# Bias strips interleaved by four heads, a compressed bias read from them, and a new order of loads and splits in front

## What is computed

```
shift, scale, gate = split(c @ mod_w[0, 0] + mod_b[0, 0])
h    = rms_norm(x, norm_w[0, 0, 0]) * (1 + scale) + shift
proj = h @ w_in_ab          # q, k, v of three branches, gates, q, k, v of the sliding window
# heads a: compressed keys (15), selected blocks, window; summed by gates
s    = q . kc * scale + rel_tab[rel_bucket(t - cmp_end)]    # compressed
s    = q . k  * scale + rel_tab[rel_bucket(t - pos)]        # selected, window
# heads b: sliding window of 128 with a sink logit, same bias, other heads of the table
o    = concat(o_a, o_b) @ w_out_ab
```

## Time and profile before

| | |
|---|---|
| median of the runs | 1017.39 us |
| profiled execution | 1018.37 us, its span 1016.6 us |
| mean granted TensorE clock | 0.986 |
| TensorE busy | 967.5 us (95%) |
| VectorE busy | 799.1 us (79%) |
| ScalarE busy | 557.8 us (55%) |
| DMA | 228.11 MB, mean 224 GB/s |

### The profile page before, as it was taken

How to read it: one execution, slowest core, us unless ns; L and a number is a source line. 1 busy time by engine, 2 the same in 40 slices (tenths; PEclk the granted TensorE clock), 3 DMA queues, 4 the chain that set the end, 5 groups by cost and what they waited for, 6 DMA issues and landing times. The chain is left out here.

```text
span 1016.6 us, 19939 instructions
## 1 busy us (share of the span) xinstructions
PE 967.5 (95%) x7814; PEld 925.4 (91%) x7814; DVE 799.1 (79%) x1436; ACT 557.8 (55%) x1130; POOL 4.8 (0%) x15
## 2 busy tenths in 40 slices
PE   8968989999999999998999999999989899999996
PEld 6757869999999989988999999999888899999995
DVE  4738997798888777888789888877877757877775
ACT  3515874554444465574545444446567457776663
POOL 0100000000000000000000000000000000000000
PEclk9979999999999999999999999999999999999999
DMA  9995776498988756822479888874722436665531
GB/s 345 358 276 178 252 254 249 176 344 321 336 294 295 260 187 219 304 80 99 172 261 330 303 306 302 288 240 183 244 80 73 166 108 185 197 193 186 181 111 42
DMA packets 63004, 228.11 MB, mean 224 GB/s; under 512 B 7091, under 2 KB 7475, under 8 KB 62806
## 3 DMA queue, kind: packets, MB, share of 16 engines
q1 hardware_dynamic: 62150, 224.55, 64.3%
q0 software_dynamic: 640, 2.10, 0.8%
q10 hardware_dynamic: 144, 0.52, 0.1%
HBM read 225.57 MB, written 1.57 MB: 223 GB/s over the span
## 5 line engine op out<-in xcount | busy, mean ns | idle before, releaser
L1935 PE MATMUL bank<-hH,wH 128*128 128x258 f32 (+1 forms) x1520 | 438.0, 288 | 6.7 <-DVE hL L1313 2.6
L1936 PE MATMUL bank<-hL,wH 128*128 128x258 f32 (+1 forms) x1520 | 431.9, 284 | 0.0
L1937 PE MATMUL bank<-hH,wL 128*128 128x258 f32 (+1 forms) x1520 | 430.3, 283 | 0.0
L1266 DVE TENSOR_TENSOR wL<-raw,wH 128x1024 fp32r<-128x1024 f32 x264 | 320.9, 1220 | 43.6 <-ACT wH L780 42.1
L1935 PEld LDWEIGHTS bank<-hH,wH 128*128 128x128 f32 x1520 | 288.8, 190 | 13.0 <-issue 6.2
L780 ACT ACTIVATE wH<-raw 128x1024 fp32r<-128x1024 f32 x264 | 270.2, 1047 | 43.8 <-DMA raw<-in_weights 22.6
L1937 PEld LDWEIGHTS bank<-hH,wL 128*128 128x128 f32 x1520 | 289.9, 191 | 0.0
L1936 PEld LDWEIGHTS bank<-hL,wH 128*128 128x128 f32 x1520 | 289.5, 190 | 0.4
L1935 PE MATMUL bank<-aH,wH 128*128 128x256 f32 x592 | 168.1, 284 | 1.3 <-DVE aL L1499 1.3
L1937 PE MATMUL bank<-aH,wL 128*128 128x256 f32 x592 | 167.6, 283 | 0.0
L1936 PE MATMUL bank<-aL,wH 128*128 128x256 f32 x592 | 167.6, 283 | 0.0
(11 more groups left out here) (335 smaller groups left out, 1038.2 us busy)
## 6 DMA issues: line engine op xcount, KB each, us to landing
raw<-in_weights SPq DMA_DIRECT2D x264, 512.0 KB, 4.6
modbuf<-in_mods SPq DMA_DIRECT2D x129, 512.0 KB, 6.4
raw<-in_mods SPq DMA_DIRECT2D x10, 512.0 KB, 11.8
strips<-bias_table POOLq DMA_DIRECT2D x8, 256.0 KB, 13.5
strips<-in_mods SPq DMA_DIRECT2D x3, 512.0 KB, 15.5
modbuf<-in_weights SPq DMA_DIRECT2D x3, 512.0 KB, 14.0
x<-in_xT SPq DMA_DIRECT2D x2, 512.0 KB, 6.7
proj<-in_mods SPq DMA_DIRECT2D x2, 512.0 KB, 15.0
```

Of the source, the lines that this page charges most:

```text
L1266: V.tensor_tensor(wL[:, slot, :], raw[:, slot, :], wH[:, slot, :].bitcast(F32), ALU.subtract).then_inc(lo_ready[c], 1)
L1935: mm(out, lhs_h, rhs_h, start=start, stop=False, skip_group_check=True)
L1936: mm(out, lhs_h, rhs_l, start=False, stop=False, skip_group_check=True)
L1937: return mm(out, lhs_l, rhs_h, start=False, stop=stop, skip_group_check=True)
```

## The change

1. `strips` goes from 8 x (256 x 2) to 4 x (256 x 4): four heads interleaved, columns of one head 16 bytes apart. The product for the table (68 rows of operand for 34, eight matmuls of 128 columns for four of 256) and POOL's eight DMAs follow (4 runs of 4 KB a partition for 8 of 2 KB).
2. The compressed bias is read from the strips, every 16th column. `hot_cmp`, `relblock`, `cmpmask`, `bc`, their loads, TensorE's 8 products and VectorE's two instructions go. POOL fills `cs` with a large value, where step 3 adds only the valid 7 and 15 columns.
3. SP: `c` and `x` first, then parameters and `rel`; the start's jobs and units in another order; the first part of the constants (with the identity) behind unit 6; `cw_values` no longer wait for the one-hot product and have a semaphore of their own. `warm` (ones) replaces the loaded ones in the first products.
4. ScalarE: the two `crow` copies go to VectorE; the table leaves behind row 4 instead of row 6; POOL's strips wait for job 11, not 15; `split_upto` stands at 8, then 9, for 7, 10, 11 and 12, and `ab_split(s)` is at most 10 + 2s.
5. VectorE: `compressed_input(1, 1)` goes into step 0; units 9 to 11 are split in the steps.
6. TensorE: other numbers and places of clock-keeping matmuls; unit 2's first columns behind those of units 0 and 1.

```diff
-        strips = sb("strips", [P, 8, S, 2])
-        bc = sb("bc", [P, QT, 16, H])
+        strips = sb("strips", [P, 4, S, 4])
...
-            return strips[:, n // 2, cols, n % 2]
+            return strips[:, n // 4, cols, n % 4]
...
-            return min(29, max(e for fill in AB_FILL[:s + 1] for e in fill) + 5)
+            return min(29, 10 + 2 * s, max(e for fill in AB_FILL[:s + 1] for e in fill) + 5)
...
-            sp.dma_start(par[:, 0:PARAM_FIRST], A["params"][:, 0:PARAM_FIRST]).then_inc(par_landed, 16)
             sp.dma_start(crow[0:1, 1, :], A["c"][0:1, :]).then_inc(c_landed, 16)
-            sp.dma_start(con[:, 0:CONST_START], A["consts"][:, 0:CONST_START]).then_inc(con_landed, 16)
-            sp.dma_start(rel, A["rel"]).then_inc(rel_landed, 16)
             for half in range(2):
...
+            sp.dma_start(par[:, 0:PARAM_FIRST], A["params"][:, 0:PARAM_FIRST]).then_inc(par_landed, 16)
+            sp.dma_start(rel, A["rel"]).then_inc(rel_landed, 16)
             load_start_job(0)
+            load_start_job(1)
             load_start_unit(0)
-            load_start_job(1)
             load_start_unit(1)
+            load_start_job(2)
+            load_start_job(3)
             load_start_job(15)
...
             load_unit(6)
-            sp.dma_start(hot_cmp, A["hot_cmp"]).then_inc(hot_landed, 16)
             sp.dma_start(par[:, PARAM_FIRST:], A["params"][:, PARAM_FIRST:]).then_inc(par_landed, 16)
-            sp.dma_start(con[:, CONST_START:CONST_FIRST], A["consts"][:, CONST_START:CONST_FIRST]).then_inc(con_landed, 16)
+            sp.dma_start(con[:, 0:CONST_FIRST], A["consts"][:, 0:CONST_FIRST]).then_inc(con_landed, 16)
...
             jobs_upto(JOBS_END["start"] + 2)
-            sp.wait_ge(misc_psum, misc["bc"] + 1)
...
+            pool.wait_ge(rstd_ready, 1)
+            nc.gpsimd.memset(cs, BIG).then_inc(cs_ready, 1)
+
             pool.wait_ge(table_out, 16)
-            pool.wait_ge(mod_used, JOBS_END["start"])
+            pool.wait_ge(mod_used, 11)
...
-                diag = bass.AP(A["table"].tensor, 2 * (P - 1 - a),
-                               [[8 * 1024 - 2 * 8, COPIES], [1024, 8], [1, 2 * S]])
+                diag = bass.AP(A["table"].tensor, 4 * (P - 1 - a),
+                               [[8 * 1024 - 4 * 8, COPIES], [2048, 4], [1, 4 * S]])
...
+                if k == 4:
+                    act.wait_ge(table_half, 1)
+                    act.wait_ge(misc_taken, misc["table"] + 1)
+                    act.dma_start(A["table"], pt[:, :, :].rearrange("p a b -> p (a b)")).then_inc(table_out, 16)
...
-            split_upto(7)
+            split_upto(8)
             for e in range(2):
                 ab_take(e)
...
-            split_upto(10)
             ab_take(6)
-            split_upto(11)
+            split_upto(9)
             act.wait_ge(misc_psum, misc["gatesT"] + 1)
             nc.scalar.activation(small[:, 0:48], bank[7][:, 0:48], ACT.Exp, scale=-1.0).then_inc(misc_taken, 1)
-            split_upto(12)
             ab_take(7)
...
+            for half in range(2):
+                dve.wait_ge(crow_psum, half + 1)
+                V.tensor_copy(crow[:, 0, half * 512:(half + 1) * 512], bank[(3, 5)[half]][:, :]).then_inc(crow_ready, 1)
+                add_pair(0, half)
...
-            take("bc")
-            dve.wait_ge(con_landed, 32)
-            link(V.tensor_scalar(bc[:, :, :, :].rearrange("p q n h -> p (q n h)"), bank[2][:, 0:S], -1.0, None,
-                                 ALU.mult))
...
-            compressed_input(1, 1)
-            split_upto(11)
             dve.wait_ge(misc_taken, misc["gatesT"] + 1)
...
-            split_upto(12)
+            dve.wait_ge(con_landed, 16)
             dve.wait_ge(strips_landed, 16 * (P // COPIES))
...
+                if s == 0:
+                    compressed_input(1, 1)
...
-                        bias = bc[:, q].rearrange("p n (g t) -> p g t n", g=G)
+                        n = (7, NCMP)[q]
...
+                        at = (1 - q) * P + CLEN - 1
+                        bias = strips[:, 0:G, at:S:CSTR, :].rearrange("p g n t -> p g t n")
                         ins = V.tensor_tensor(dst, src, bias, ALU.add)
...
-            misc_free("bc")
-            keep_clock(bank[2], 6)
+            misc_free("gates")
+            keep_warm(bank[2], 3)
...
-            pe.wait_ge(hot_landed, 16)
-            pe.wait_ge(par_landed, 32)
-            hot = hot_cmp.rearrange("p (g q) -> p g q", g=4)
-            for q in range(QT):
-                for g in range(4):
-                    last = mm(bank[2][:, q * P + g * 32:q * P + (g + 1) * 32], hot[:, g, q * P:(q + 1) * P],
-                              param("relblock"), start=True, stop=True, skip_group_check=True)
-            last.then_inc(misc_psum, 1)
             ab_project(6)
+            misc_free("gates")
```

More of the change, by code:

```diff
@@ L62 @@
 _c = 0
-for _name, _n in (("ident", P), ("ones", P), ("cmpmask", QT * 16), ("rowvalid", QT), ("select", P), ("headmask", H),
+for _name, _n in (("ident", P), ("ones", P), ("rowvalid", QT), ("select", P), ("headmask", H),
                   ("blockones", P), ("rot", P), ("tri", P), ("neg1", P), ("cos", S), ("sin", S),
@@ L150, in shape_constants @@
     put("headmask", (i[:, None] // 16 == np.arange(H)[None]).astype(np.float32))
[L151 to L154, removed]
     far = 255 - np.arange(512)
-    rel = np.zeros((REL + 2, 768), np.float32)
+    rel = np.zeros((REL + 2, 512), np.float32)
     rel[rel_bucket(far), np.arange(512)] = -1.0
-    rel[REL, 0:512] = far < 0
-    rel[REL + 1, 0:512] = far >= 128
-    return c, hot_cmp, rel
+    rel[REL] = far < 0
+    rel[REL + 1] = far >= 128
+    return c, rel
 class Count:
@@ L266, in build_program @@
         ttf = tt.rearrange("p k s -> p (k s)")
[L267 to L268 removed]
+        rel = strips[0:2 * (REL + 2), 0, :, :].rearrange("p s j -> p (s j)")[:, 0:S + 4 * P]
         par_landed = sem("par_landed")
@@ L390, in build_program @@
         NORMS = ["A0", "B0", "A1", "B1", "A2", "B2", "A3", "B3", "A4", "A5", "A6"]
-        MISC = ["table", "bc", "gates", "gatesT", "cmpk", "cmpv", "vrep", "cscore"]
+        MISC = ["table", "gates", "gatesT", "cmpk", "cmpv", "vrep", "cscore"]
         misc = {name: i for i, name in enumerate(MISC)}
@@ L1534, in first_low @@
                                 ALU.subtract).then_inc(h_ready, 1)
-            for b in range(4):
-                add_pair(0, b)
+            add_pair(0, 2)
+            add_pair(0, 3)
             jobs_upto(1)
@@ L1949, in sum_square @@
                     pe.wait_ge(pair_ready, 4 * PAIRED.index(n) + b + 1)
-                    mm(bank[6][:, 0:S], ones, buf[:, 0:S], start=(b == 0), stop=(b == 3),
+                    mm(bank[6][:, 0:S], warm if n == 0 else ones, buf[:, 0:S], start=(b == 0), stop=(b == 3),
                        skip_group_check=True).then_inc(sq_used, 1)
@@ L2183, in _, with keep_warm @@
             pe.wait_ge(warm_ready, 1)
-            for _ in range(5):
-                mm(bank[0][:, 384:512], warm, warm, start=True, stop=True, skip_group_check=True)
-            pe.wait_ge(con_landed, 16)
+            def keep_warm(bk, n):
+                for _ in range(n):
+                    mm(bk[:, 384:512], warm, warm, start=True, stop=True, skip_group_check=True)
+            keep_warm(bank[0], 5)
             pe.wait_ge(c_landed, 16)
             for half in range(2):
-                mm(bank[(3, 5)[half]][:, :], const("ones", 1), crow[0:1, 1, half * 512:(half + 1) * 512], start=True, stop=True,
+                mm(bank[(3, 5)[half]][:, :], warm[0:1, :], crow[0:1, 1, half * 512:(half + 1) * 512], start=True, stop=True,
                    skip_group_check=True).then_inc(crow_psum, 1)
@@ L2193, in _ @@
             for half in range(2):
-                out = bank[(2, 7)[half]][:, :].rearrange("p (n j) -> p n j", j=2)
-                for j in range(2):
-                    last = mm(out[:, :, j], rel[:, 512 + j * P:512 + (j + 1) * P], rel[:, half * S:(half + 1) * S], start=True, stop=True,
+                out = bank[(2, 7)[half]][:, :].rearrange("p (n j) -> p n j", j=4)
+                for j in range(4):
+                    last = mm(out[:, :, j], rel[:, S + j * P:S + (j + 1) * P], rel[:, half * P:(half + 1) * P], start=True, stop=True,
                               skip_group_check=True)
             last.then_inc(misc_psum, 1)
-            keep_clock(bank[0], 2)
+            keep_warm(bank[0], 4)
             pe.wait_ge(par_landed, 16)
@@ L2202, in _ @@
                 first_columns(e, 0)
+            keep_warm(bank[0], 4)
             pe.wait_ge(rstd_ready, 1)
             shift_product(15)
-            first_columns(2, 0)
-            keep_clock(bank[0], 3)
-            for e in range(3):
+            for e in range(2):
                 first_columns(e, 1)
-            first_values(0)
-            first_values(1)
-            misc_free("bc")
-            keep_clock(bank[2], 6)
+            for k in range(2):
```

(24 more changed lines are left out.)

46 lines of the change are left out of this document (16 added, 30 removed).

## The result

The changed kernel took 1022.59 us, median of six runs (1019.83 to 1025.43), beside 1017.82 for the kernel before: ratio 1.0047, 95% interval 1.0028 to 1.0067. It is slower by 4.8 us, where 3.5 faster was forecast. The profiled execution took 1025.43 us (span 1023.6, mean clock 0.976).

What follows compares the result with a forecast made beforehand. The prediction took VectorE as the bound from 90 us on, with late weight units and loads holding the head. It summed -9.9 + 5.4 + 1.0 = -3.5 us to 1013.9 us against the median, range 1006 to 1018.

Steps and rivals of the forecast that it cites:

- TensorE's hole: TensorE's 9.7 us wait before the first scores goes through new split limits; scores start at about 55.7 for 65.10.
- The stream's end: SP's stream of loads in the head ends at 72.7 us, where the queues were full to 77 before.
- 4 KB pieces: Strip DMAs in 4 KB pieces for 2 KB move faster in the head: -1.0 us, at worst nothing.
- the sum of -4.2: All changes to the head's loads together bring the stream's end forward by 4.2 us, between 1.5 and 7.
- It lands at 72.7 + 1.2 = 73.9: Job 17, queued behind SP's stream, lands 1.2 us after the stream's end, at 73.9; VectorE started it at 83.37 before.
- The constants that move or grow: +0.2: In the head's loads, the table operand growing from 102 to 204 KB, less two small tables, costs 0.2 us.
- Strips before 60: A sign that the forecast is right: the strips land before 60 us in the head.
- the 9.9: Gain on VectorE's schedule at the end of step 4's scores, 93.3 for 103.2: 9.9 us if nothing else changes.
- From job 17 to step 4's end: VectorE's stretch from job 17 to step 4's scores: 19.9 us, less a 2.5 wait, plus 2.4 of splits, less 0.35.
- The layout's cost: Negated scores read at 16 bytes cost VectorE 5.4 us over 20 first-mixer heads, 1.0 in the second layer's MoBA heads.
- B: Rival: VectorE's strip reads at a 16-byte step are free, so 9.9 us are kept: 1007.5 us; chance 0.32.
- C: Rival: strips and table write slow SP's stream; 2.7 us won, 6.4 lost to the layout: 1021.1 us; chance 0.12.

Runs made afterwards that it cites:

- e7: The kernel before with the new split order alone, loads, table and layout unchanged: 1015.20 us, ratio 0.9973 to the kernel before.
- e8: e1 with SP waiting for job 17's landing before it issues job 18 and unit 16: ratio 0.9957 to the kernel before.
- e13: e1 with the table product's operand padded with zero rows to the four-head layout's 204 KB, from 102: ratio 0.9977 to the kernel before.
- e1: The changed kernel with the strips back at two heads interleaved (8 bytes, 2 KB pieces, smaller table operand): 1012.89 us, ratio 0.9951 to the kernel before.
- e2: The kernel before with only the layout of four heads interleaved, including its doubled table operand: 1026.99 us, ratio 1.0086 to the kernel before.
- e3: e1 with VectorE's second compressed_input and splits of units 9 to 11 ahead of its wait for the strips: ratio 0.9955 to the kernel before.
- e4: The changed kernel with POOL's DMAs moving only half the strips, heads 0 to 7: 1019.64 us in a single run.
- e11: The changed kernel with the compression's weights loaded over all 128 partitions: 1018.17 us, ratio 1.0002 to the kernel before.
- e5: e1 with the compression's weights loaded by three DMAs over 128 partitions for six over 64: 1006.86 us, ratio 0.9887 to the kernel before.
- e10: The kernel before with only the compression's weights loaded over all 128 partitions: 1015.12 us, ratio 0.9971 to the kernel before.
- e9: e1 with the old split order, the new loads and earlier table kept: 1016.40 us, ratio 0.9981 to the kernel before.

## Why the prediction was wrong

**TensorE's hole** went as forecast: first scores at 55.10 for "about 55.7". By itself that wins nothing (the stretch at 1.2 GHz only moved by 4 us); what it wins goes through job 15 and job 17, as argued, and e7 shows it.

**The stream's end** was right with the old operand. 72.7 was forecast; in e8 the full rate ends at 74.4 with job 17's 1.2 us in it, so at 73.2. It got there without the 4 KB pieces, whose -1.0 e13 shows to be nothing, so the sum of -4.2 is right in part by luck. Gap, bytes and order I have not tried one by one.

**"It lands at 72.7 + 1.2 = 73.9" failed.** This is the first step that failed: the bytes' time is not the landing. A load is there only when its last packets are, 3.2 us behind the end of the full rate (e8). A bound for it was shown: job 17, issued at 78.62, had landed by 83.37. These 4.75 us are no landing time, for VectorE came to it from a split and did not wait; but I took 1.2 and had no row for the rest.

**"The constants that move or grow: +0.2" failed too.** The doubled table operand, priced at its bytes, costs 2.0 us at job 17 (e13 against e1) in the new order of loads, and none is seen in the old one (e2).

**Strips before 60** was wrong (64.82), and it did not matter (e3), for VectorE's next need is job 17.

**A term that was missing.** I read the gain on VectorE's schedule alone. In e1 job 17 is 3.7 us behind the forecast 73.9, which would leave 6.2 of the 9.9; its first mixer ends 4.9 sooner. Between, at 82 to 95 us, TensorE of e1 is 12.18 of 13 us busy at 1.2 GHz, and VectorE waits 1.6 us at 106.1 for the high part of a unit (e3 shows both too). In e13, whose job 17 is 2.0 later, the clock is back sooner, there is no such wait, and the first mixer ends only 0.45 us behind e1's. First e1, then e13:

```profile
82.00:95.00 13.00, 12.18 (x58) 9.23 (x60) 12.53 (x38) 7.10 (x25) 0.00 (x0) 0.51 0.47 163
```

```profile
82.00:95.00 13.00, 10.40 (x77) 7.84 (x77) 12.69 (x41) 8.38 (x24) 0.00 (x0) 0.87 0.60 201
```

Why the clock was low for longer in e1 is open.

**From job 17 to step 4's end** I took 19.9 - 2.5 + 2.4 - 0.35 = 19.45 us. Measured 20.38, which holds six heads' layout cost, 1.7, counted elsewhere. The -0.35 in it does not follow from its own numbers (80 of 256 columns of 0.76 us are 0.24); measured, the two additions take 258 and 373 ns for 375 and 386, 0.13 us less. So the 9.9 us shrink by 3.2 and 2.0 to 4.7, and e13's first mixer ends 4.5 us sooner; with what is said of e1 above, the fit is in part chance.

**The layout's cost, "5.4 + 1.0", was the third term that failed**, right in mechanism and short in size. Against e13 the changed kernel is level up to step 2 (83.2 in both: steps 0 and 1 do lie in the slack), 5.4 us behind at step 11 (18 heads x 0.28 = 5.0 of it) and 7.4 at the mixer's end, where 5.4 was counted. The last step's heads are 0.6 of the difference. In the rest TensorE's granted clock fell, which it did not in e13; 150 to 160 us in the changed kernel and in e13:

```profile
150.00:160.00 10.00, 7.96 (x54) 7.26 (x53) 8.26 (x15) 4.60 (x11) 0.00 (x0) 0.83 0.72 261
```

```profile
150.00:160.00 10.00, 10.00 (x86) 9.54 (x85) 7.31 (x12) 4.11 (x6) 0.00 (x0) 1.00 0.98 360
```

TensorE, waiting more for VectorE, was 7.96 us busy for 10.00, and part of that stretch ran at 1.2 GHz. That the late heads cause this is not shown: from step 11 to the mixer's end it is 27.9 us here and 28.0 in e2, but 26.5 in e4 and 26.4 in e11, with four heads too, and 26.0 in e13. In the MoBA heads I counted 1.0 of 2.2 us; between the two `rstd` around that layer's attention (387.85 to 497.75 before, 390.76 to 503.21 after) it is 2.55, and 2.3 in e2: all of it.

**The sum by what was measured**: -4.5 + 7.4 + 2.5 = +5.4; the medians differ by 4.8. The profiled execution itself stands 7.1 above its counterpart; the other 1.5 lie in the third block, which reads no strips: between two of its `rstd` (713.11 and 819.98 before) it took 106.9 us before and 108.4 after, 108.0 in e1 and 105.2 in e5, so that is the spread of single runs.

**The rivals.** B is out: the step is not free. C gave 1021.1, near the time measured, but that is luck: its terms (2.7 won, 6.4 lost) are both short of the measured 4.5 and 9.9, and its mechanism is not what happened, for e1 has the strips beside units 7 to 9 and the table ahead of the last jobs, and wins 5 us. What was measured, a landing's tail, a load that slows its neighbours and a layout dearer than 6.4, was in no rival.

## What to carry to other kernels

Price a load on the path by a row from its issue to the start of a user that waited for it, not by bytes over rate. Where the queues are busy all the time at half the rate, look at the shape of what is in flight before its order: here six narrow DMAs cost 6.5 us in e1, more than the whole reordering won (5.0), though only 3.0 in the kernel before. And a layout read by the bound engine in every step is to be priced at every one of its reads, before its one-time saving.

## What the runs showed of the hardware

- With six DMAs to 64 partitions among the loads, the busy queues moved 211 GB/s at 50 to 56 us; with three DMAs over 128 partitions for the same weights, 315 (e1, e5).
- A load of 68 rows of 3 KB in place of 34 lowers the rate at 6 to 10 us from about 355 to 257 to 297 GB/s and sets the stream back by 1.0 us there, for 0.24 us of bytes; at job 17 it is 2.0 (e1, e13).
- fp32 on VectorE at a step of 16 bytes costs 0.72 to 0.77 ns a column over the 1.05 at 8 bytes, about the 0.74 at 32 bytes.
- The tail of a full stream, from the first fall of the rate to its last packets, took 1.5 to 3.5 us (e10, before, e9, e8); in e8 the last load's user started 3.2 us behind the end of the full rate.
